# Differential attention with blocks in the order 3, 0, 1, 2, two sets of score banks and the rotation's additions on GpSimd; beside it minima, a folded final norm and an early load

## The chip, the core and the metric

The kernel runs on one core of one Trainium2 chip. The metric is the device time of one launch in microseconds (us). All engines of the core work from queues of their own: TensorE (PE in the rows; PEld is its weight load), VectorE (DVE), ScalarE (ACT), GpSimd (POOL) and SyncE (SP), which only issues transfers here. PEclk in the profile is the granted clock of TensorE as a share of 2.4 GHz, so 0.5 is its lower level of 1.2 GHz.

## The reference

The program is a stack of three model blocks on 512 tokens of width 1024 in float32. Three places in it matter here.

In the first block, 16 meta tokens stand ahead of the 512. Its differential attention has 8 heads; each head has two score maps over the same values, whose difference weighs the values:

```python
s = jnp.einsum('bhqd,bhkd->bhqk', qb, k, preferred_element_type=f32)
s = jnp.where(pos[None, :] <= qpos[:, None], s, neg)
pr = jax.nn.softmax(s, axis=-1).reshape(bsz, DIFF_HEADS, 2, nq, seqlen)
attn_w = pr[:, :, 0] - lam * pr[:, :, 1]
return jnp.einsum('bhqk,bhkd->bhqd', attn_w.astype(v.dtype), v)
```

Queries come in 4 blocks of 128, and q and k are rotated first (`partial_rope`). The second block has a sparse attention (NSA) with three branches per group of queries: compressed keys (31 of them), selected keys, and a window. Each is a softmax with a bias, and the three outputs are added with gates. The third block ends with the whole program's last step, `rmsnorm(x, g_final_3)`: x times the inverse root of its mean square over 1024 channels, times a weight.

## The kernel before

The program is a row of stages. Each stage has its own semaphores and ends in a barrier over all engines. Matmul layers run in `chain`, which takes a list of jobs, streams weight slabs of 512 KB through a ring of buffers, splits each slab into a high and a low part (`whi` on ScalarE, `wlo` on VectorE) and gathers three products per tile in PSUM. A slab can be loaded into a buffer of its own, `ahead`, during the chain before, so that the next chain starts at once; the first chain that uses `ahead` issues this load itself, at its start (L195).

`diff_attention` (L1536 on) works through 8 heads of 4 query blocks, 32 steps `a`. Keys of block b are 16 + 128(b + 1) wide: 144, 272, 400, 528. The two maps e = 0, 1 of a head lie in rows 0 to 63 and 64 to 127 of the rotated operands `rot`. PSUM has two banks for each map (`ps_s[e]`, banks A and B). All engines follow one written order, `lagging()`: a head is five slots, first the rotation of its q and k (`swaps`, L1608, a matmul with a permutation) with the transposition of its values (`values`, L1615), then the four blocks in the order 0, 1, 2, 3. In the slot of step a, TensorE does `scores(a)` (S: L1629 for the 16 meta keys, L1632 for the rest), then `turn(a2)` (T: transposes of weights, L1640 and L1642) for the slot two before, then `weigh(a3)` (Wg: weights times values, L1651 and L1653) for three before. VectorE does `maxima` (M: L1761 takes scores plus mask out of PSUM and the row maximum `top`; L1766 turns the two maxima into the exponent's bias `low`), and one slot later `weights` (W: L1771 to L1778). ScalarE does `powers` (exponent, L1695) and the copies out of PSUM. For the rotation GpSimd multiplies by cosines (L1736, L1737), VectorE multiplies the swapped operand by sines (L1749) and adds the two (L1753). Every block's scores start at the same place, so each pair of score matmuls waits until VectorE has taken the pair before it:

```python
for e in range(2):
    pe.wait_ge(top_ready[e], a)
```

`nsa_attention` (L2096 on) has 48 steps p, three per group. VectorE does the same reduction with a bias (L2276) and `low` (L2280), ScalarE the exponents (`powers`, L2231) and its half of the copies of transposed weights (`turned_weights`, L2239 and L2241); TensorE's transposes (L2169, L2172) wait for both engines' copies of the step before. VectorE joins the three branches (L2302 to L2308).

`rmsnorm` (L491 on) is a stage of its own after the last chain: 8 squares on ScalarE, a sum over channels by matmuls with ones (L542, two halves of each of 8 tiles), mean and root, a reciprocal (L556), 8 products (L559), each followed by its transfer to the output.

Of the kernel before, what the change touches and what calls it, by code (L numbers as in the profile page):

```python
# [12 lines left out]
P = 128  # L13
BANK = 512
# [44 lines left out]
class Job:  # L59
# [15 lines left out]
    def makes_pair(self, n):  # L75
        return self.kind in ("join", "relu2") or (self.kind == "ffn" and n % 2 == 1) or self.fold is not None


class Ahead:


    def __init__(self, nc, memory):
        self.nc, self.memory, self.loaded, self.times = nc, memory, nc.alloc_semaphore("ahead_loaded"), 0

    def take(self):
        if self.times == 0:
            self.place = self.memory.enter_context(self.nc.sbuf_tensor("ahead", [P, 8, P], F32, side="right"))
        self.times += 1
        return self.place, self.loaded, self.times


class Fold:
# [3 lines left out]
    def __init__(self, pair, cols, eps, inner=None, eps_inner=None):  # L96
        self.pair, self.cols, self.eps, self.inner, self.eps_inner = pair, cols, eps, inner, eps_inner

# [5 lines left out]
def chain(nc, ones, jobs, T, norm, pending=None, ring=4, side=None, loads=(), taps=None, restore=None, ahead=None,  # L104
# [39 lines left out]
    for s, f in folds:  # L144
        per = 7 * (2 if f.inner is not None else 1)
        sum_no[s], summed_total = (summed_total, summed_total + per), summed_total + per
        fold_job[s] = slabs[s - 1][0]
    two_norms = any(f.inner is not None for f in stat_at.values())
# [11 lines left out]
    with stage(nc) as s_:  # L160
# [18 lines left out]

        first_in = wbuf[0]  # L180
# [10 lines left out]
        with nc.Block() as block:  # L191
            @block.sync
            def _(sp):
                if ahead is not None and ahead[2] == 1:
                    sp.dma_start(first_in[:], jobs[0].w[0, 0]).then_inc(ahead[1], 16)  # L195
# [9 lines left out]
                if following is not None:  # L205
                    sp.wait_ge(lo_ready, (S - 1) // ring * ring + 1)
                    n = following.shape[3] // -(-following.shape[3] // 8)
                    sp.dma_start(first_in[:, 0:n, :], following[0, 0, :, 0:n, :]).then_inc(ahead[1], 16)

            @block.tensor  # L210
            def _(pe):
# [9 lines left out]
                for s, (j, n, i) in enumerate(slabs):  # L221
# [23 lines left out]
                    if side is not None:  # L245
                        side.pe(pe, s, stat)

            @block.scalar
            def _(act):
# [19 lines left out]
                def folded(f, n, x):  # L269
                    copy(f.pair[0][n], x, ACT.Copy, scale=f.cols[:, n:n + 1]).then_inc(hi_done, 1)  # L270
# [57 lines left out]
                if loads:  # L328
                    act.wait_ge(arrived, 16 * len(loads))

            @block.vector
            def _(dve):
# [28 lines left out]
                def folded(f, n, x, last):  # L361
                    no = sum_no[last][0]
                    dve.wait_ge(hi_done, part["made", fold_job[last], n])
# [78 lines left out]
                for s, (j, n, i) in enumerate(slabs):  # L442
# [12 lines left out]
                    if side is not None:  # L455
                        side.dve(dve, s)

# [31 lines left out]


def rmsnorm(nc, ones, x, weight, out, T, eps, src=None, dst=None):  # L491

    pair = isinstance(out, tuple)
    K = x.shape[1]
    nh, th = halves(T)
    with stage(nc) as s:
        w = s.sb("norm_w", [P, K])  # L500
        sq = s.sb("squares", [P, K, T])
        rstd = s.sb("rstd", [P, T])
        acc = s.ps("sum_squares", [P, nh, BANK])
        loaded, squared, summed = s.sem("loaded"), s.sem("squared"), s.sem("summed")
        mean_ready, root_ready, order, stored = s.sem("mean_ready"), s.sem("root_ready"), s.sem("order"), s.sem("stored")
        ready, hi_ready = s.sem("normed"), s.sem("hi_ready")

        whole = sq if pair else out
        acc_v = acc[:, :, 0:th]
        rstd_v = rstd[:].rearrange("p (h t) -> p h t", h=nh)  # L510
        with nc.Block() as block:  # L511
            @block.sync
            def _(sp):
                sp.dma_start(w[:], weight).then_inc(loaded, 16)
                if src is not None:
                    for k in range(K):
                        sp.dma_start(x[:, k, :], src[:, k, :]).then_inc(loaded, 16)
                if dst is not None:
                    for k in range(K):
                        sp.wait_ge(ready, k + 1)  # L520
                        sp.dma_start(dst[:, k, :], out[:, k, :]).then_inc(stored, 16)
# [3198 lines left out]
```

## Time and profile before

| | |
|---|---|
| Median of 3 runs | 3665.03 us (3663.76 to 3668.27) |
| The profiled execution | 3664.28 us |
| Its span | 3662.5 us |
| Mean granted clock | 0.952 |
| Busy | PE 92%, PEld 75%, DVE 55%, ACT 34%, POOL 6% |
| 731.9 to 856: score loop of differential attention | PE busy 105.4 of 124.2 us |
| 1645 to 1783: NSA attention | PE busy 122.8 of 138.0 us |
| 3638 to 3662.5: the program's end | PE busy 9.0 of 24.5 us |

The time of an execution is that of the launch, and the span is from the first to the last instruction that the profile holds. Busy times of an engine over the whole span mix stages with different limits, so the three stretches that the change touches stand apart.

### The profile page before, as it was taken

The numbers are of one execution on the slowest core, as the hardware profiler recorded it, in microseconds if no ns is written. First come the engines' busy times: TensorE is split into PE (matmuls) and PEld (weight loads), VectorE is DVE, ScalarE is ACT, GpSimd is POOL, SyncE is SP. The second block draws the span as 40 slices with busy tenths as digits, with TensorE's granted clock in tenths as the row PEclk, the third lists the DMA queues.
The fourth block names the chain that finished last, engine by engine and source line by source line (L and its number), as shares of the span: only waits on it lengthen the run. The fifth ranks groups of instructions, "written<-read, shape, count | busy, mean of one in ns | idle before, by whom it ended". The sixth has DMA issues, their size and how long they took to land. (4 is left out here: it accounts for less than half of the span.)

```text
span 3662.5 us, 57266 instructions
## 1 busy us (share of the span) xinstructions
PE 3359.4 (92%) x24193; PEld 2748.0 (75%) x24193; DVE 2023.8 (55%) x3286; ACT 1230.1 (34%) x2142; POOL 212.6 (6%) x174
## 2 busy tenths in 40 slices
PE   7988999988999999888999998979699889999998
PEld 6988888856888887656677776857578587878886
DVE  4885564564355344577546776356736545464342
ACT  4552323254333233214433222234412234333231
POOL 2323230010000000000000000000100020000000
PEclk9998998998999999999999999989799789999999
DMA  4431103101222222620122222312022003232221
GB/s 148 154 134 57 43 23 111 58 1 58 98 92 92 98 92 75 158 61 13 47 81 92 86 87 92 102 52 95 11 92 95 1 2 110 79 106 98 95 95 57
DMA packets 99462, 287.84 MB, mean 79 GB/s; under 512 B 19738, under 2 KB 23962, under 8 KB 97160
## 3 DMA queue, kind: packets, MB, share of 16 engines
q1 hardware_dynamic: 93104, 269.43, 21.6%
q10 hardware_dynamic: 6104, 14.75, 1.6%
q8 instruction: 193, 3.16, 0.4%
q14 instruction: 61, 0.50, 0.0%
HBM read 264.22 MB, written 19.89 MB: 78 GB/s over the span
## 5 line engine op out<-in xcount | busy, mean ns | idle before, releaser
L240 PE MATMUL acc<-h_hi,whi 128*128 128x512 f32 x1992 | 800.3, 402 | 64.8 <-DVE wlo L432 42.4
L240 PE MATMUL acc<-h_hi,wlo 128*128 128x512 f32 x1992 | 791.3, 397 | 0.0
L240 PE MATMUL acc<-h_lo,whi 128*128 128x512 f32 x1928 | 770.0, 399 | 0.0
L240 PEld LDWEIGHTS acc<-h_hi,whi 128*128 128x128 f32 x1992 | 379.1, 190 | 175.3 <-DVE wlo L432 44.7
L338 DVE TENSOR_TENSOR wlo<-wbuf,whi 128x1024 fp32r<-128x1024 f32 (+3 forms) x277 | 318.6, 1150 | 273.4 <-ACT whi L256 271.1
L240 PEld LDWEIGHTS acc<-h_hi,wlo 128*128 128x128 f32 x1992 | 379.3, 190 | 87.9
L240 PEld LDWEIGHTS acc<-h_lo,whi 128*128 128x128 f32 x1928 | 366.7, 190 | 86.1 <-issue 2.9
L256 ACT ACTIVATE whi<-wbuf 128x1024 fp32r<-128x1024 f32 (+3 forms) x277 | 274.5, 991 | 348.1 <-PE acc L240 318.3
L240 PE MATMUL acc<-arena_round,whi 128*128 128x512 f32 x736 | 236.4, 392 | 4.8 <-DVE arena_round L398 4.8
L338 DVE TENSOR_TENSOR wlo<-ahead,whi 128x1024 fp32r<-128x1024 f32 (+3 forms) x132 | 152.3, 1154 | 139.9 <-ACT whi L256 139.2
L256 ACT ACTIVATE whi<-ahead 128x1024 fp32r<-128x1024 f32 (+3 forms) x132 | 131.4, 995 | 174.1 <-PE acc L240 167.7
L240 PEld LDWEIGHTS acc<-arena_round,whi 128*128 128x128 f32 x736 | 139.3, 190 | 34.6 <-DVE arena_round L398 5.6
L240 PE MATMUL acc<-arena_round,wlo 128*128 128x512 f32 x416 | 162.8, 391 | 0.0
L672 PE MATMUL acc<-h_hi,whi 128*128 128x264 f32 x480 | 141.4, 295 | 7.5 <-POOL wlo L660 7.5
L240 PE MATMUL acc<-gates_round,whi 128*128 128x512 f32 x384 | 141.2, 395 | 3.0 <-DVE gates_round L398 1.8
L404 DVE TENSOR_TENSOR x<-acc,x 128x512 f32<-128x512 f32 x64 | 44.3, 691 | 178.2 <-PE acc L240 178.2
L672 PE MATMUL acc<-h_hi,wlo 128*128 128x264 f32 x480 | 137.0, 286 | 0.0
L672 PE MATMUL acc<-h_lo,whi 128*128 128x264 f32 x480 | 137.0, 285 | 0.0
L240 PE MATMUL acc<-gates_round,wlo 128*128 128x512 f32 x320 | 125.4, 392 | 0.0
L289 ACT ACTIVATE val<-tmp 128x512 f32<-128x512 f32 x64 | 40.5, 633 | 216.7 <-DVE tmp L400 216.7
L2837 POOL MEMSET scores<- 128x2048 f32 x1 | 1.8, 1809 | 1768.6 <-POOLq L42 1768.6
L1433 PE MATMUL acc<-h_hi,whi 128*128 128x264 f32 x336 | 103.1, 307 | 1.4 <-DVE wlo L1473 1.4
(752 smaller groups left out, 6349.4 us busy)
## 6 DMA issues: line engine op xcount, KB each, us to landing
wbuf<-in_mlp_out SPq DMA_DIRECT2D x46, 512.0 KB, 3.3
wbuf<-in_mlp_in SPq DMA_DIRECT2D x45, 512.0 KB, 3.2
wbuf<-in_w_gates SPq DMA_DIRECT2D x38, 512.0 KB, 3.3
wbuf<-in_ffn_up SPq DMA_DIRECT2D x29, 512.0 KB, 3.2
wbuf<-in_w_qkv SPq DMA_DIRECT2D x22, 512.0 KB, 3.3
rwkv_factors<-factors SPq DMA_DIRECT2D x8, 1320.0 KB, 4.6
ahead<-in_mlp_in SPq DMA_DIRECT2D x19, 512.0 KB, 3.2
wbuf<-in_w_rwkv SPq DMA_DIRECT2D x18, 512.0 KB, 5.5
```

The source lines that it names most:

```text
L240: mm = nc.tensor.matmul(acc[t % NB][:, 0:T], wt[s % ring][:, k - a, :], xt, start=(kx == 0 and q == 0), stop=(kx == job.K - 1 and q == 2))
L256: copy(whi[s % ring][:, 0:size(s), :], wbuf[s % ring][:, 0:size(s), :], ACT.Copy).then_inc(hi_ready, 1)
L289: copy(val[t % 2][:], tmp[t % 2][:], ACT.Square)
L338: TT(wlo[s % ring][:, 0:size(s), :], wbuf[s % ring][:, 0:size(s), :], whi[s % ring][:, 0:size(s), :].bitcast(F32), ALU.subtract).then_inc( ...
L404: TT(job.dst[n], ps, job.other[n], ALU.add).then_inc(evicted_d, 1)
L672: mm = nc.tensor.matmul(acc[n % 2][:, hf, 0:H], wt[n % R][:, kx, :], xt[:, kx, at], start=(kx == 0 and q == 0), stop=(kx == 7 and q == 2))
L1433: mm = nc.tensor.matmul(acc[n % NB][:, h, 0:H], wt[n % R][:, k, :], xt[:, k, h * H:(h + 1) * H], start=(k == 0 and q == 0), stop=(k == 7 a ...
L2837: nc.gpsimd.memset(scores[:], 0.0).then_inc(cleared, 1)
```

## The change

1. `diff_attention` takes the blocks of a head in the order 3, 0, 1, 2. `place` puts scores at three different starts, so that block 3 takes both banks, 0 bank A, 1 bank B, 2 bank A; a step waits for the block that used its bank last. The rotation of the next head no longer has a slot of its own: it is issued behind the last block's scores of this head and uses bank B alone. The 16 meta keys and values of all heads are rotated and transposed once, at the start (`metas`, `rope_meta`). GpSimd, not VectorE, adds the rotation's two parts.
2. In both attentions the reduction multiplies by minus the scale and takes the minimum, which is the bias itself, so `low` is gone.
3. In `nsa_attention` ScalarE does the copies of step p-2 ahead of the exponents of step p.
4. The `rmsnorm` stage is gone. The last chain takes the squares, their sums and the product with the weight (`Ending`) as it finishes each tile of its last job; what is left behind it is one matmul with ones, mean, root, reciprocal and 8 products, six on VectorE and two on GpSimd.
5. The first use of `ahead` is loaded by `diff_attention`'s SyncE, a stage earlier. The buffer exists from the start, and the program asks for less scratch for DMA descriptors to make room.

```diff
-                    for e in range(2):
-                        h = slice(64 * e, 64 * e + 64)
-                        nc.tensor.matmul(ps_s[e][:, LO:BANK], r[h, 0, j * P:(j + 1) * P], r[h, 1, 0:M], start=True, stop=True)
-                    for e in range(2):
-                        h = slice(64 * e, 64 * e + 64)
-                        nc.tensor.matmul(ps_s[e][:, BANK:LO + keys(a)], r[h, 0, j * P:(j + 1) * P], r[h, 1, M:keys(a)],
-                                         start=True, stop=True).then_inc(sc_ready[e], 1)
+                        h, to = slice(64 * e, 64 * e + 64), place(e, a)
+                        q = r[h, 0, b * P:(b + 1) * P]
+                        free = a if a % NJ < 2 else a - 1
+                        if free > 0:
+                            pe.wait_ge(least_ready[e], free)
+                        nc.tensor.matmul(to[:, 0:M], q, meta[h, i, :], start=True, stop=True)
+                        nc.tensor.matmul(to[:, M:keys(a)], q, r[h, 1, 0:keys(a) - M], start=True, stop=True).then_inc(sc_ready[e], 1)
...
+                swaps(0)
+                metas()
+                values(0)
+                for a in range(NA + 3):
+                    if a < NA:
                         scores(a)
-                    elif i is not None:
-                        swaps(i)
-                        values(i)
-                    if a2 is not None:
-                        turn(a2)
-                    if a3 is not None:
-                        weigh(a3)
+                    if a < NA - 1 and a % NJ == NJ - 1:
+                        swaps(head(a) + 1)
+                        values(head(a) + 1)
+                    if 2 <= a < NA + 2:
+                        turn(a - 2)
+                    if a >= 3:
+                        weigh(a - 3)
...
+                    for e in range(2):
+                        pool.wait_ge(cos_done, 2 * i + e + 1)
+                        pool.wait_ge(sin_done, 2 * i + e + 1)
+                        nc.gpsimd.tensor_tensor(r[:, e, :], r[:, e, :], swapped[e][:], ALU.add).then_inc(rope_done, 1)
...
-                for i, a, a1, _, _ in lagging():
-                    if a is not None:
+                rope(0)
+                rope_meta()
+                for a in range(NA + 1):
+                    if a < NA:
                         maxima(a)
-                    elif i is not None:
-                        rope(i)
-                    if a1 is not None:
-                        weights(a1)
+                    if a < NA - 1 and a % NJ == NJ - 1:
+                        rope(head(a) + 1)
+                    if a >= 1:
+                        weights(a - 1)
...
-                        nc.vector.tensor_tensor_reduce(out=pr[e][p % 3][:, 0:n], in0=ps_s[e][p % 2][:, 0:n], in1=b, scale=1.0, scalar=3 * NEG,
-                                                       op0=ALU.add, op1=ALU.max, accum_out=top[e][:, p:p + 1]).then_inc(top_ready[e], 1)
-                    for e in range(2):
-                        dve.wait_ge(top_ready[e], p + 1)
-                        TS(low[e][:, p:p + 1], top[e][:, p:p + 1], -1.0, None, ALU.mult).then_inc(max_ready[e], 1)
+                        nc.vector.tensor_tensor_reduce(out=pr[e][p % 3][:, 0:n], in0=ps_s[e][p % 2][:, 0:n], in1=b, scale=-1.0, scalar=-3 * NEG,
+                                                       op0=ALU.add, op1=ALU.min, accum_out=least[e][:, p:p + 1]).then_inc(least_ready[e], 1)
...
+                if ending is not None:
+                    no = len(stat_at) + 1
+                    dve.wait_ge(stat_ready, no)
+                    TS(scale[:], stat[0][:, 0:T], 1.0 / (8 * P), ending.eps, ALU.mult, ALU.add).then_inc(var_ready, 1)
+                    dve.wait_ge(root_ready, no)
+                    nc.vector.reciprocal(scale[:], scale[:]).then_inc(scale_ready, 1)
+                    dve.wait_ge(scale_ready, no)
+                    dve.wait_ge(scaled, 8)
+                    for k in by_dve_last:
+                        TT(ends_on[k], ends_on[k], scale[:], ALU.mult).then_inc(last_normed, 1)
```

TensorE's queue before, in the middle of differential attention, from the scores of a head's block 3 to the next head's first transposes (`ps_s<-rot` are scores, `rope_swap` the rotation, `ps_v<-ident,p` the values, `ps_m`, `ps_t<-ident,wt` the T, `ps_o` the Wg):

```order
L1629 MATMUL ps_s<-rot 128x16 x2
L1632 MATMUL ps_s<-rot 128x512 x2
L1640 MATMUL ps_m<-ident,wt 16x128
L1642 MATMUL ps_t<-ident,wt 128x128 x2
L1651 MATMUL ps_o<-vtm,wTm 128x128
L1653 MATMUL ps_o<-vt,wT 128x128
L1608 MATMUL ps_s<-p_next,rope_swap 128x512
L1607 MATMUL ps_s<-p,rope_swap 128x16
L1608 MATMUL ps_s<-p,rope_swap 128x512
L1613 MATMUL ps_s<-ident,p 16x128
L1615 MATMUL ps_v<-ident,p 128x128 x4
L1640 MATMUL ps_m<-ident,wt 16x128
```

The same place in the changed kernel, from the rotation to the second block of the new head:

```order
L1588 MATMUL ps_s<-p_next,rope_swap 128x512
L1588 MATMUL ps_s<-p,rope_swap 128x512
L1594 MATMUL ps_v<-ident,p 128x128 x4
L1620 MATMUL ps_m<-ident,wt 16x128
L1622 MATMUL ps_t<-ident,wt 128x128
L1631 MATMUL ps_o<-vtm,wTm 128x128
L1633 MATMUL ps_o<-vt,wT 128x128 x4
L1610 MATMUL ps_s<-meta,rot 128x16
L1611 MATMUL ps_s<-rot 128x512
L1610 MATMUL ps_s<-meta,rot 128x16
L1611 MATMUL ps_s<-rot 128x512
L1620 MATMUL ps_m<-ident,wt 16x128
```

The rotation now has one whole T and the Wg of block 3 behind it before the next head's scores, the 16-column pieces in it are gone, and the new head starts with the 512-wide scores; the meta part of each map stands right ahead of its main part.

ScalarE's queue before, in the middle of NSA attention, over one group (`pr,total` are exponents, `wT<-ps_t` copies of transposed weights, `o_plain` an output):

```order
L2231 ACTIVATE pr,total<-pr,low 128x384 x2
L2241 ACTIVATE wT<-ps_t 128x256
L2231 ACTIVATE pr,total<-pr,low 128x384 x2
L2239 ACTIVATE wT<-ps_t 31x128
L2231 ACTIVATE pr,total<-pr,low 128x31 x2
L2241 ACTIVATE wT<-ps_t 128x384
L2247 ACTIVATE o_plain<-ps_o 128x128
```

The same place now:

```order
L2244 ACTIVATE o_plain<-ps_o 128x128
L2228 ACTIVATE pr,total<-pr,least 128x31 x2
L2238 ACTIVATE wT<-ps_t 128x256
L2228 ACTIVATE pr,total<-pr,least 128x384 x2
L2236 ACTIVATE wT<-ps_t 31x128
L2228 ACTIVATE pr,total<-pr,least 128x384 x2
L2238 ACTIVATE wT<-ps_t 128x384
```

Each copy stands one step's exponents earlier.

GpSimd's queue at the start of differential attention now:

```order
L1724 TENSOR_TENSOR rot<-p_next,rope_cos 128x512
L1724 TENSOR_TENSOR rot<-p,rope_cos 128x512
L1727 TENSOR_TENSOR meta<-p,rope_cos 128x16 x8
L1731 TENSOR_TENSOR rot<-rot,swapped 128x512 x2
L1724 TENSOR_TENSOR rot<-p_next,rope_cos 128x512
```

Before, it held the two `rot<-p,rope_cos` of each head and nothing else; the eight small products and the two additions per head are new.

## Rows read from the trace of the kernel before

**Rows 1.** Windows: score loop of differential attention (length, busy by engine, clock, DMA).

```profile
731.85:856.00 124.15, 105.38 (x643) 67.00 (x643) 84.06 (x317) 72.38 (x291) 15.24 (x12) 0.93 0.00 1
```

**Rows 2.** Timeline of TensorE, one head: start, length, what, [idle before].

```profile
779.74 0.40 PE L1629 MATMUL ps_s<-rot 64*128 64x16 f32 x4
...
781.07 0.28 PE L1640 MATMUL ps_m<-ident,wt 128*16 128x128 f32 x1 [0.61 <-DVE wt L1778]
...
783.85 0.48 PE L1651 MATMUL ps_o<-vtm,wTm 16*128 16x128 f32 x2
...
785.35 0.40 PE L1629 MATMUL ps_s<-rot 64*128 64x16 f32 x4
...
786.42 0.28 PE L1640 MATMUL ps_m<-ident,wt 128*16 128x128 f32 x1
...
787.85 0.40 PE L1629 MATMUL ps_s<-rot 64*128 64x16 f32 x4 [1.05 <-DVE top L1761]
...
789.60 0.27 PE L1640 MATMUL ps_m<-ident,wt 128*16 128x128 f32 x1 [0.39 <-ACT wT L1704]
...
790.75 1.02 PE L1608 MATMUL ps_s<-p,rope_swap 128*128 128x512 f32 x2
791.61 0.29 PE L1607 MATMUL ps_s<-p,rope_swap 128*128 128x16 f32 x2
...
792.70 0.27 PE L1613 MATMUL ps_s<-ident,p 128*16 128x128 f32 x1
...
793.24 0.27 PE L1640 MATMUL ps_m<-ident,wt 128*16 128x128 f32 x1
...
794.88 0.40 PE L1629 MATMUL ps_s<-rot 64*128 64x16 f32 x4
```

**Rows 3.** Timeline of VectorE, the same head, its last block and the next rotation.

```profile
789.32 0.71 DVE L1761 CUSTOM_DVE_ANT_0 sc<-ps_s,mask 128x528 f32<-128x528 f32 x1 [0.37 <-PE ps_s L1632]
...
790.58 0.27 DVE L1766 TENSOR_SCALAR low<-top 128x1 f32<-128x1 f32 x2
...
791.40 0.92 DVE L1778 SCALAR_TENSOR_TENSOR wt<-sc,share 128x400 f32<-128x400 f32 x1
792.25 1.36 DVE L1749 TENSOR_TENSOR swapped<-ps_s,rope_sin 128x512 f32<-128x512 f32 x2
```

**Rows 4.** Timeline of VectorE, a later head, with GpSimd idle.

```profile
836.17 0.15 DVE L1771 RECIPROCAL inv<-total 128x1 f32<-128x1 f32 x1
...
836.80 0.63 DVE L1778 SCALAR_TENSOR_TENSOR wt<-sc,share 128x400 f32<-128x400 f32 x1
```

**Rows 5.** Timeline of GpSimd, the first of a head's two products with the cosines.

```profile
789.36 1.27 POOL L1736 TENSOR_TENSOR rot<-p,rope_cos 128x512 f32<-128x512 f32 x1 [12.59 <-PE ps_s L1632]
```

**Rows 6.** Timeline, the end of differential attention: last scores and last output copy.

```profile
850.25 1.14 PE L1632 MATMUL ps_s<-rot 64*128 64x512 f32 x4
...
864.14 0.27 ACT L1709 ACTIVATE unscaled<-ps_o 128x128 f32<-128x128 f32 x1
```

**Rows 7.** Timeline, start of the next chain: first load, first use.

```profile
878.01 0.33 SPq L195 DMA_DIRECT2D ahead<-in_w_gates  x1
...
881.33 1.33 ACT L303 ACTIVATE whi<-ahead 128x256 fp32r<-128x256 f32 x4 [4.20 <-DMA ahead<-in_w_gates]
```

**Rows 8.** Waits, 1638 to 1800. Who waits for whom: us in total, times, longest.

```profile
PE ps_t L2172 <- ACT wT L2239: 9.7, 10, 1.2
...
PE ps_t L2169 <- ACT wT L2241: 4.7, 11, 0.7
```

**Rows 9.** Timeline of VectorE, the last eviction.

```profile
3638.17 0.69 DVE L404 TENSOR_TENSOR x<-acc,x 128x512 f32<-128x512 f32 x1 [10.19 <-PE acc L240]
```

**Rows 10.** The chain that ended last, from 3600 on: start, length, what.

```profile
3640.49 8.85 PE sum_squares L542 x16
...
3650.74 3.36 DVE rstd L556
...
3655.55 3.98 DVE x L559 x6
```

More of the change, by code:

```diff
@@ L75, in makes_pair @@
     def makes_pair(self, n):
-        return self.kind in ("join", "relu2") or (self.kind == "ffn" and n % 2 == 1) or self.fold is not None
+        return self.kind in ("join", "relu2") or (self.kind == "ffn" and n % 2 == 1) or isinstance(self.fold, Fold)
 class Ahead:
     def __init__(self, nc, memory):
-        self.nc, self.memory, self.loaded, self.times = nc, memory, nc.alloc_semaphore("ahead_loaded"), 0
+        self.loaded, self.times = nc.alloc_semaphore("ahead_loaded"), 0
+        self.place = memory.enter_context(nc.sbuf_tensor("ahead", [P, 8, P], F32, side="right"))
     def take(self):
-        if self.times == 0:
-            self.place = self.memory.enter_context(self.nc.sbuf_tensor("ahead", [P, 8, P], F32, side="right"))
         self.times += 1
@@ L208, in _ @@
                     sp.dma_start(first_in[:, 0:n, :], following[0, 0, :, 0:n, :]).then_inc(ahead[1], 16)
+                if ending is not None:
+                    for k in range(8):
+                        if k in by_dve_last:
+                            sp.wait_ge(last_normed, by_dve_last.index(k) + 1)
+                        else:
+                            sp.wait_ge(last_pool, 1 if k == 3 else 2)
+                        sp.dma_start(ending.dst[:, k, :], ends_on[k]).then_inc(last_stored, 16)
+                    sp.wait_ge(last_stored, 16 * 8)
+            @block.gpsimd
+            def _(pool):
+                if ending is not None:
+                    pool.wait_ge(scale_ready, len(stat_at) + 1)
+                    pool.wait_ge(scaled, 8)
+                    for k in (3, 6):
+                        nc.gpsimd.tensor_tensor(ends_on[k], ends_on[k], scale[:], ALU.mult).then_inc(last_pool, 1)
             @block.tensor
@@ L246, in _ @@
                         side.pe(pe, s, stat)
+                if ending is not None:
+                    pe.wait_ge(summed, sum_no[S][1])
+                    nc.tensor.matmul(stat[0][:, 0:T], ones[:], sums[0][:], start=True, stop=True).then_inc(stat_ready, 1)
             @block.scalar
@@ L269, in folded @@
                 def folded(f, n, x):
+                    if f is ending:
+                        copy(sums[0][:] if n == 0 else sqx[n % 2][:], x, ACT.Square).then_inc(sq_done, 1)
+                        copy(x, x, ACT.Copy, scale=f.cols[:, n:n + 1]).then_inc(scaled, 1)
+                        return
                     copy(f.pair[0][n], x, ACT.Copy, scale=f.cols[:, n:n + 1]).then_inc(hi_done, 1)
@@ L329, in _ @@
                     act.wait_ge(arrived, 16 * len(loads))
+                if ending is not None:
+                    act.wait_ge(var_ready, len(stat_at) + 1)
+                    copy(scale[:], scale[:], ACT.Sqrt).then_inc(root_ready, 1)
             @block.vector
```

247 lines of the change are left out of this document (101 added, 146 removed).

## The prediction

> **What bounds the kernel now.** I first read the page: TensorE is busy for 92% of the span, so a change is worth only what it takes from TensorE's work or its waits. Then I cut out the stretches that the change touches. In the score loop of differential attention TensorE is busy for 105.4 of 124.2 us, at nine tenths of its clock [rows 1]; in NSA attention for 122.8 of 138.0 (the table above); after 3638 it is nearly idle. No engine is full in the first two; the order of waits sets the pace.
>
> One head shows it [rows 2]. It lasts 794.88 - 779.74 = 15.14 us, and TensorE is idle for 0.61 (waiting for VectorE's weights), 1.05 (for the maxima, that is for the only set of banks) and 0.39 (a copy): 2.05, which leaves 13.09 of its own steps. A step's cost is the distance to the next start, less its idle: S of block 3 is 789.60 - 0.39 - 787.85 = 1.36; T of block 1 and Wg of block 0 together 790.75 - 789.60 = 1.15; a rotation matmul 0.86; Wg of block 3 785.35 - 783.85 = 1.50; T of block 0 787.85 - 1.05 - 786.42 = 0.38; S of block 0 781.07 - 0.61 - 779.74 = 0.72.
>
> **Differential attention, the head.** Two 16-column rotations (0.29, one row, and only one of the pair of operands has it, so 0.14) and one of the five transposes of the values (793.24 - 792.70 = 0.54, so 0.11 each) leave each head: 13.09 - 0.25 = 12.84. Now the new waits, by walking through the four steps:
> - Block 3's pair fills both banks, so block 0's scores wait until VectorE has read it. VectorE starts 0.11 after TensorE's step is over and takes 790.58 - 789.32 = 1.26 [rows 3]; TensorE starts again about 0.23 after a maximum (787.85 shows no more). That is 1.60, and the T and Wg between cover 1.15: idle 0.45.
> - The T after it needs W of block 2, which VectorE does behind that maximum: 836.80 + 0.63 - 836.17 = 1.26 [rows 4], so it is ready 1.37 + 1.26 + 0.12 = 2.75 after the scores of block 3, and TensorE is there after 1.60 + 0.72 = 2.32: idle 0.43.
> - Blocks 1 and 2 find a bank free; I count nothing.
> - The next head needs its rotation. After S of block 2 TensorE does 2 x 0.86 + 0.44 + 0.38 + 1.50 = 4.04. VectorE's maximum of block 2 (528 columns take 1.26, so 400 by width 0.96) ends at 1.1, the two sine products (0.68 each [rows 3]) at 1.8 and 2.5. GpSimd's two additions, priced as its product of the same size, 1.27 [rows 5] and back to back, run from 1.9 to 4.4: idle 0.4 to 0.5.
>
> The head becomes 12.84 + 0.45 + 0.43 + 0.45 = 14.15, 1.0 less. Over the 7 boundaries this saves 7. The two `low` add nothing to it: TensorE's wait for the bank ends with the maximum, before them, and so does the wait counted here; they only shorten the way to the exponent.
>
> **Its ends.** From the last scores of block 3 (850.25 + 1.14) to the last output copy (864.14 + 0.27) pass 13.0 us, at half clock [rows 6]. The last block is now block 2 of 400 keys, with its long predecessor four steps back. M, exponent, W, T, copies and Wg of block 3 are each a quarter to a fifth longer than those of block 2, and the small blocks' steps wait in the shade of it; I take 3, bounds 0 and 4. At the start 16 small matmuls of the meta keys and values stand ahead of the first scores, at half clock, and GpSimd's eight products beside them: I take 1.2 lost, bounds 0.5 and 2.5. Together the part saves 7 + 3 - 1.2 = 9, bounds 0 and 14.
>
> **The price of the additions.** GpSimd's product is 1.27 where VectorE's like it is 0.68, and VectorE's weights of 400 keys take 0.92 beside that product [rows 3] and 0.63 with GpSimd idle [rows 4]. So the two cost each other something like 0.3 where they meet. Now GpSimd's additions meet W of block 1, which has two operands in SBUF. The Trainium skill's SBUF — State Buffer ("two separate sides") goes further: it calls the shared port pair an exclusive lock, which the second one waits for until the first is done. Its GPSIMD Engine Reference (4.1, Engine selection) advises against two-input elementwise work there, at about half the speed. By that rule the second addition ends some 0.5 later and the head boundary costs 0.9, not 0.45. The trace agrees with half speed; whether a whole instruction waits, it doesn't show.
>
> **NSA attention.** TensorE's idle time there is almost all one kind: its transposes wait for ScalarE's copy of the step before, 9.7 + 4.7 us in 21 waits [rows 8]. The copy stands behind the exponents of a younger step, and these behind `low`. The change puts the copy first and drops `low`. The copy's own input is ready long before (TensorE wrote it a step earlier), so it runs when TensorE needs it. What is late next is VectorE: its half of the copies, and in the small groups of the joined branches, where its many short instructions fill the step. I take 12 of 14.4, with bounds 5 (half of the first row) and 15. What ScalarE's exponents lose by standing behind a copy of 0.3 to 0.6 is hidden: they have most of a step until TensorE turns them.
>
> **The program's end.** The last eviction ends at 3638.17 + 0.69 = 3638.86 [rows 9]. Now follow a square (0.7), an addition to the sums (0.7), one matmul with ones (two halves, 8.85 / 8 = 1.1), mean and root (3650.74 - 3640.49 - 8.85 = 1.4) and the reciprocal with its gap, 3.4 [rows 10]: 3646.15. The reciprocal stays whole on the path. Six products of VectorE took 3.98; two of GpSimd's (1.27) run beside them and slow them: all side by side it is 4.0, all one after another 6.5, and I take 5.6, as the weights' 0.92 against 0.63 says that they don't share freely. From the last product's end, 3659.53, to the end of the span are 2.95 now, and stay. The end comes at 3646.15 + 5.6 + 2.95 = 3654.7 instead of 3662.5: 7.8 saved, bounds 6.9 and 9.4; I count 8. Before that, squares and weight products (ScalarE) and sums (VectorE) lie beside matmuls of tiles of 8 slabs; if that cover failed, a late tile's 0.7 would show once.
>
> **The early load.** The next chain's first use of its slab waits from 877.1 for a transfer issued at 878.01, until 881.33 [rows 7]. Issued a stage earlier it is there; ScalarE can start when the transfer was issued before: 3.3 saved, bounds 2.5 and 5, as TensorE's half clock at that chain's start begins and ends earlier with it. The transfer itself, 512 KB in a stage that moves nothing else, costs nothing; smaller descriptor scratch has no queue that uses it here.
>
> **The sum.** 9 + 12 + 8 + 3.3 = 32.3. The profiled execution was 3664.28, its span 1.8 less, and the median of the runs is 0.75 above it. 3664.28 - 32.3 + 0.75 gives 3632.7; I say 3632.5. With the bounds of the terms not all at one end, its own range is 3627 to 3638.
>
> **Rivals.**
> - *The two maps no longer run side by side.* Map 0 and 1 use different halves of the rows, and their two 512-wide matmuls together take 1.14 (the row merges four pieces) [rows 6], where one of full height takes 0.86 each time. The new code puts the meta piece of map 1 between them. If that makes them queue, the pair of block 3 costs 1.72 instead of 1.36 and the head 1.3 more in its four pairs: +10, 3643. Against it: the piece uses map 1's own rows. Chance 0.10.
> - *NSA moves its wait.* VectorE's copy and join take the place of ScalarE's copy, and only 4 of 14.4 are gained: +8, 3640.5. For it: VectorE is busy for most of the small steps. Chance 0.11.
> - *GpSimd is late.* If the second addition first waits for VectorE's weights, which is up to 0.63 [rows 4], or if each takes half as long again as the product's 1.27, the boundary costs 0.6 to 1.3 more, 7 times, 4 to 9: 3637 to 3642, say 3640. For it: the additions end 0.4 after TensorE is there even undisturbed. Chance 0.09. The lock that the Trainium skill's SBUF — State Buffer states would be one way to it.
> - *More is gained.* All of NSA's waits, 9.4 at the end, the small drain, the clock kept through: 3622 to 3626. Chance 0.13.
> - *Slower.* The fused reduction with a minimum and a scale other than 1 stands nowhere in this trace. Were that form to take twice the time, VectorE's four reductions (1.26 for 528 columns, by width 3.2 for the 1344 of a head) would add 3.2 to a head, most of it on the way from bank to bank: +23 for 8 heads, and in NSA, where 48 such pairs stand ahead of the exponents, some +15 and the 12 not gained. That ends at 3682; the sign turns where the form takes about 1.8 times as long. Against it: it is the same instruction with other operators. Chance 0.04.
> - *No change to be measured:* several of the losses at once, 0.03.
>
> **Chances and range.** 0.2% is 7.3 us, about what a measurement of this kernel tells from no change. The forecast has 0.50. Faster by over 0.2% are it, the first three rivals and the fourth, 0.93; within 0.03; slower 0.04. The range takes in the forecast and the first three, 0.80, less their tails, and the upper edge of the fourth: 3623 to 3645.
>
> **What would show it.** TensorE's timeline of a head: a period near 14.15, idle about 0.45 ahead of L1610 of block 0, of the second T, and of the new head; that last one's releaser would be GpSimd's L1731. GpSimd's L1731 at 1.27, and L1724 as before. The custom reduction on VectorE still 0.71 for 528 columns. In NSA no wait of L2166 or L2169 on ScalarE over 3 us in sum. The first slab's `whi` within 1 us of the chain's first instruction. From the last eviction to the end of the span, 16 us. The prediction fails if a head stays at 15, if the reduction is longer, or if NSA's waits come back under another name.

## The result, and the profile after

The changed kernel takes 3659.66 us (median of 11 runs, 3653.32 to 3663.76), the kernel before 3665.6 (median of 11 runs beside it). The ratio is 0.9979, with a 95% interval of 0.997 to 0.9989: 6 us less and not 32. The profiled execution took 3653.76 us, with a span of 3652.0 and a mean granted clock of 0.945, where it was 0.952 before.

Matched points of the two traces say where the time went. Windows of the differential attention, from its first dummy matmul to the first `whi` of the next chain, first of the kernel before, then of the changed one (stretch, length, busy and count of PE, PEld, DVE, ACT and POOL, granted clock, DMA share, GB/s):

```profile
722.95:881.33 158.38, 129.14 (x756) 86.22 (x756) 97.40 (x362) 84.23 (x316) 20.27 (x16) 0.89 0.02 6
```

```profile
716.23:893.13 176.90, 162.36 (x756) 107.56 (x756) 87.14 (x284) 84.29 (x311) 42.50 (x40) 0.72 0.01 4
759.30:766.00 6.70, 5.95 (x40) 4.07 (x39) 4.60 (x15) 4.21 (x18) 3.85 (x3) 1.00 0.00 0
766.00:776.50 10.50, 10.50 (x38) 6.56 (x39) 3.38 (x13) 4.82 (x19) 0.00 (x0) 0.51 0.01 2
776.50:800.30 23.80, 21.45 (x136) 14.16 (x134) 17.02 (x49) 14.53 (x60) 10.29 (x8) 1.00 0.00 1
800.30:810.50 10.20, 10.20 (x34) 5.93 (x34) 3.30 (x12) 4.16 (x16) 0.21 (x1) 0.50 0.00 0
```

The stage has become 18.5 us longer, not 12 shorter, and TensorE, busy for 162 instead of 129 us, did nothing more for it: each of the two traces holds 756 matmuls. What changed is the granted clock, 0.72 instead of 0.89 (0.93 in the loop alone [rows 1]). The last four rows show the pattern: stretches at 2.4 GHz of 7 to 24 us, and between them some at 1.2 GHz, of 10 to 14 us, in which TensorE is busy without a gap. `ending_on_vector` below has the same attention and shows the loss a second time: 176.3 us at 0.73.

The timeline of TensorE in the changed kernel shows the moment at which the clock falls, and behind it a head at the higher level (779.96 to 794.33):

```profile
763.49 0.39 PE L1610 MATMUL ps_s<-meta,rot 64*128 64x16 f32 x2
...
765.29 0.27 PE L1620 MATMUL ps_m<-ident,wt 128*16 128x128 f32 x1 [0.75 <-ACT wT L1686]
...
765.82 0.59 PE L1631 MATMUL ps_o<-vtm,wTm 16*128 16x128 f32 x2
766.34 1.22 PE L1633 MATMUL ps_o<-vt,wT 128*128 128x128 f32 x4
767.49 0.62 PE L1610 MATMUL ps_s<-meta,rot 64*128 64x16 f32 x4
767.94 1.21 PE L1611 MATMUL ps_s<-rot 64*128 64x256 f32 x4
...
779.96 0.41 PE L1610 MATMUL ps_s<-meta,rot 64*128 64x16 f32 x4 [0.40 <-POOL rot L1731]
...
782.51 0.39 PE L1610 MATMUL ps_s<-meta,rot 64*128 64x16 f32 x2
...
784.31 0.27 PE L1620 MATMUL ps_m<-ident,wt 128*16 128x128 f32 x1 [0.75 <-ACT wT L1686]
...
794.33 0.41 PE L1610 MATMUL ps_s<-meta,rot 64*128 64x16 f32 x4 [0.44 <-POOL rot L1731]
```

At the higher level a head lasts 794.33 - 779.96 = 14.37 us, against 15.14 before [rows 2]: the step I had at 14.15. Two waits are left, 0.40 to 0.44 for GpSimd's addition and 0.75 for a copy of ScalarE's. At 765.82 `L1631 x2` takes 0.59, and at 766.34 `L1633 x4` takes 1.22; at full clock they take 0.48 and 0.71: the clock has fallen just behind the scores of block 0, the idle 0.75 and the transposes of block 2. It falls six times in the score loop, near 745.6, 766.0, 800.3, 817.3, 837.8 and 858.3, each time 4 to 6 us behind the first scores of a head, in this idle time or up to 2 us behind it. (The expectation of `old_attention` below counts five.) In the kernel before it falls once in the loop, near 835.8, for 3 us, and in `old_attention`, which has the old order, twice for as long (773.0 and 790.0).

VectorE and GpSimd around a head's boundary, timelines of the changed kernel:

```profile
793.02 1.55 DVE L1773 SCALAR_TENSOR_TENSOR wt<-sc,share 128x272 f32<-128x272 f32 x1
795.83 0.71 DVE L1759 CUSTOM_DVE_ANT_0 sc<-ps_s,mask 128x528 f32<-128x528 f32 x1 [1.25 <-PE ps_s L1611]
```

```profile
791.78 2.50 POOL L1731 TENSOR_TENSOR rot<-rot,swapped 128x512 f32<-128x512 f32 x2 [9.23 <-DVE swapped L1743]
```

The reduction with a minimum takes 0.71 for 528 columns, as the maximum did [rows 3]. GpSimd's additions take 1.25 each, as priced. But VectorE's weights of 272 columns take 1.55 here, 1.15 to 1.55 at all seven boundaries, and 0.50 on average before: they end at 794.57, just behind the second addition at 794.28.

The other parts: from the first transposes of NSA's stage (L2198, now L2195) to TensorE's first wait of 4.83 us in the chain behind it there were 1987.71 - 1638.62 = 349.1 us before and are 1982.88 - 1647.55 = 335.3 now, 13.8 less, and none of the waits of [rows 8] is left. From the last eviction's end to the end of the span there were 3662.5 - 3638.86 = 23.6 us [rows 9] and are 3652.0 - 3633.99 = 18.0. The timeline of the changed kernel's end:

```profile
3633.30 0.69 DVE L446 TENSOR_TENSOR x<-acc,x 128x512 f32<-128x512 f32 x1 [8.80 <-PE acc L265]
...
3635.44 1.12 PE L274 MATMUL stat<-sums,ones 128*128 128x512 f32 x2 [2.17 <-DVE sums L403]
...
3641.37 5.83 DVE L508 TENSOR_TENSOR x<-x,scale 128x512 f32<-128x512 f32 x6
3641.42 3.44 POOL L233 TENSOR_TENSOR x<-x,scale 128x512 f32<-128x512 f32 x2 [638.47 <-DVE scale L504]
3642.09 6.42 SPq L224 DMA_DIRECT2D out_features<-x  x8
```

The first use of the early load, in the changed kernel's timeline:

```profile
893.13 1.33 ACT L335 ACTIVATE whi<-ahead 128x256 fp32r<-128x256 f32 x4 [0.93 <-PEq L42]
```

ScalarE waits for no transfer there [rows 7], only for the barrier.

The remaining difference of the two spans lies ahead of the stage: the changed kernel's profiled execution is 6.7 us earlier at its start (716.23 against 722.95), where the code is the same. In the fourteen profiles of this document the stage starts between 716.2 and 725.0, so the difference goes with the execution; this one is 6 us below its own kernel's median.

### The profile page after: what moved, and what is told of

It is laid out like the page before. It is cut to its first block and busy times, and to the rows that moved or that the text cites. A ratio compares the mean times of both kernels' runs of the same rounds, so it can differ in the third digit from the quotient of the medians.

```text
span 3652.0 us, 57058 instructions
## 1 busy us (share of the span) xinstructions
PE 3375.8 (92%) x24179; PEld 2759.1 (76%) x24179; DVE 2014.1 (55%) x3117; ACT 1237.2 (34%) x2144; POOL 236.2 (6%) x200
## 5 line engine op out<-in xcount | busy, mean ns | idle before, releaser
L373 DVE TENSOR_TENSOR wlo<-ahead,whi 128x1024 fp32r<-128x1024 f32 (+3 forms) x132 | 152.3, 1154 | 133.0 <-ACT whi L284 132.3
```

The lines of the kernel that those rows point to most:

```text
L373: TT(wlo[s % ring][:, 0:size(s), :], wbuf[s % ring][:, 0:size(s), :], whi[s % ring][:, 0:size(s), :].bitcast(F32), ALU.subtract).then_inc( ...
```

## The experiments

My theory after the traces: the new order of the attention lets the granted clock fall, and this costs what the change gains. The rivals: the time is lost elsewhere, or the clock falls for something else in the new attention. A table of all runs first; "stage" is the same stretch as above, from the profile of each. Each ratio is to runs of the kernel before beside it, with its 95% interval.

| kernel | median, us | ratio | stage, us | clock in it |
|---|---|---|---|---|
| before | 3664 to 3667 | 1 | 158.4 | 0.89 |
| changed | 3659.7 | 0.9979 (0.997 to 0.9989) | 176.9 | 0.72 |
| old_attention | 3640.1 | 0.9927 (0.9915 to 0.9939) | 159.5 | 0.86 |
| copy_first | 3635.5 | 0.9919 (0.9903 to 0.9936) | 150.4 | 0.86 |
| filled_idle | 3629.0 | 0.9896 (0.9883 to 0.9909) | 146.5 | 0.92 |
| one_dummy | 3639.3 | 0.9932 (0.9917 to 0.9947) | 156.6 | 0.84 |
| moved_dummies | 3644.6 | 0.9941 (0.9926 to 0.9955) | 163.7 | 0.81 |
| order_3210 | 3622.5 | 0.9877 (0.9862 to 0.9892) | 136.9 | 0.94 |
| additions_on_vector | 3626.3 | 0.9885 (0.9869 to 0.9901) | 142.0 | 0.92 |
| combined | 3623.4 | 0.9881 (0.9866 to 0.9896) | 142.7 | 0.93 |
| best_copies | 3620.3 | 0.9876 (0.9861 to 0.9891) | 138.8 | 0.93 |
| best_additions | 3616.5 | 0.9864 (0.9847 to 0.988) | 132.3 | 0.96 |
| nsa_exponents_first | 3632.7 | 0.991 (0.9895 to 0.9925) | 137.2 | 0.94 |
| ending_on_vector | 3657.9 (one run) | | 176.3 | 0.73 |

**Is it the attention?** `old_attention` puts the function of before back, with one line more, the early load:

```diff
                 sp.dma_start(weight[:], subln).then_inc(loaded, 16)
+                sp.dma_start(ahead.place[:], following[0, 0]).then_inc(ahead.loaded, 16)
```

> The changed kernel with differential attention as before the change (block order, one set of banks, maxima, additions on VectorE), but with the early load in it; NSA, the end and the load stay changed. Theory 1 (the clock): the new order of the attention makes the granted clock fall to its lower level five times in the score loop (0.72 over the stage after the change, 0.93 before), which costs about 28 us; with the old one the stage is 158.4 - 3.3 = 155 us from its first dummy matmul to the next chain's first whi instead of 176.9, and the program takes 3659.7 - 20 = 3640. Rival (the missing time is spread over the program and differs by execution): 3655 to 3662, no change.

It took 3640.1, as the theory had it: the loss is in this one stage, and with the old attention the other parts bring 26 us together (3666.4 for the kernel before beside these runs). The stage itself was 159.5 and not 155, at a clock of 0.86 instead of 0.89; that the clock took back what the early load gives is my reading, which one execution doesn't prove.

**Is it the clock?** `filled_idle` puts three dummy matmuls of 512 columns where TensorE is idle:

```diff
                     if a < NA:
                         scores(a)
+                    if a < NA and a % NJ == 1:
+                        warm(nc, ps_s[0][:, BANK:2 * BANK], busy, 3)
```

> The changed kernel with three dummy matmuls of 512 columns (0.23 us each at full clock) behind the scores of block 0 in each of the 8 heads, in the idle 0.75 us, into a bank that is free there; no wait is changed and no result used. Theory 1a (the clock falls for want of TensorE's activity in that stretch): the clock holds, the period of a head stays 14.4, and the time falls by nearly all of the 28 us, to 3632. Rival 1b (the clock falls for another reason, such as the 64-row scores or the 16-wide pieces of the meta tokens): the time stays at 3660 or rises by up to 5, since at the lower clock the dummies take twice as long and there is no idle time to hide them.

The timeline of TensorE in `filled_idle`:

```profile
791.54 0.41 PE L1610 MATMUL ps_s<-meta,rot 64*128 64x16 f32 x4 [0.43 <-POOL rot L1733]
...
794.09 0.39 PE L1610 MATMUL ps_s<-meta,rot 64*128 64x16 f32 x2
...
795.07 0.98 PE L56 MATMUL ps_s<-h_hi 128*128 128x512 f32 x3
795.90 0.27 PE L1620 MATMUL ps_m<-ident,wt 128*16 128x128 f32 x1
...
805.91 0.41 PE L1610 MATMUL ps_s<-meta,rot 64*128 64x16 f32 x4 [0.43 <-POOL rot L1733]
```

More work, no wait removed, a head of 14.37 as in the changed kernel (791.54 to 805.91), the same two waits but one filled, and 31 us less in all. The stage went from 176.9 to 146.5: this is the price of the clock's falls in the loop, 30.4 us, shown by one edit that touches nothing else. The clock holds from the second head to the last.

**How much must there be, and where?** `one_dummy` has one in the same place instead of three:

> The changed kernel in its own order 3, 0, 1, 2 with one dummy matmul of 512 columns per head in the idle time behind the scores of block 0, instead of three. If the light stretch is only a little too light (the clock falls in it in some heads and not in others): one dummy holds the clock in most heads, 3630 to 3638. If it is far too light: the clock falls nearly as often as without, 3650 to 3660.

`moved_dummies` has the three at the other end of the head, in the wait for the rotation:

```diff
+                    if 0 < a < NA and a % NJ == 0:
+                        pe.wait_ge(least_ready[0], a)
+                        warm(nc, ps_s[0][:, 0:BANK], busy, 3)
                     if a < NA:
                         scores(a)
```

> The changed kernel with the same three dummy matmuls of 512 columns per head, but at the other end of the head: ahead of the scores of block 3, where TensorE waits 0.44 us for the rotation. Theory 1e (the chip looks at each short stretch by itself, so the light stretch around the scores of block 0 must be filled): the clock falls about as often as without them, and each head costs 0.3 more, 3655 to 3664. Rival 1f (what counts is the activity of the head as a whole): it holds as with the dummies in the idle time, 3630 to 3635.

One dummy took 3639.3, 1 us above what the first theory gave; the three at the other end took 3644.6, which lies between what the two theories gave. Three dummies in the one place (0.9896) and in the other (0.9941) are clear of each other's intervals, so the place matters; the moved ones also made a head 14.57 (764.29 to 778.86) instead of 14.37, up to 1.4 us in all. One dummy in the first place and three in the second aren't told apart by their times. In the traces the clock still fell in the loop three times with one dummy and four times with the moved ones (whose profiled execution, 3651.8, was their slowest), against six, and each time 5 to 7 us behind the first scores of a head. That the moved ones help at all says that the stretch around block 0's scores doesn't decide alone; what else counts, no run here shows.

**Is it the idle time or the order?** `copy_first` shortens the idle time without new work, by putting ScalarE's copy ahead of the exponents:

```diff
+                    if 2 <= a < NA + 2:
+                        turned_weights(a - 2)
                     if a < NA:
                         powers(a)
                     if a < NA - 1 and a % NJ == NJ - 1:
                         values(head(a) + 1)
-                    if 2 <= a < NA + 2:
-                        turned_weights(a - 2)
```

> The changed kernel with one edit on ScalarE in differential attention: the copies of the weights of step a-2 stand ahead of the exponents of step a. This takes away the idle 0.75 us that TensorE has after the scores of block 0 in each head, while it waits for such a copy. Theory 1a (the clock falls because the small blocks' steps and this idle time lie next to each other): a head of 14.36 becomes 13.6 and the clock holds through most of the loop: 3659.7 - 28 - 6 = 3626. Rival 1b (the clock falls by the new order whatever waits there): only the waits at full clock are saved, 2 to 4 us, 3656. Rival 2 (exponents come late behind the copies): no gain or a loss of up to 5.

It came out between theory and rival, 3635.5, and with the widest spread of all runs, 3626.4 to 3649.7. Of its six executions the slowest has a mean granted clock of 0.946 over the program and the fastest 0.954, so the spread goes with the clock. A wait of 0.49 is left, now for VectorE's weights (in this kernel's timeline):

```profile
791.35 0.41 PE L1610 MATMUL ps_s<-meta,rot 64*128 64x16 f32 x4 [0.44 <-POOL rot L1731]
...
795.44 0.28 PE L1620 MATMUL ps_m<-ident,wt 128*16 128x128 f32 x1 [0.49 <-DVE wt L1773]
...
805.47 0.41 PE L1610 MATMUL ps_s<-meta,rot 64*128 64x16 f32 x4 [0.43 <-POOL rot L1731]
```

A head is 14.12 at full clock, and in this trace the clock still fell twice in the loop, again behind the scores of block 0. `order_3210` changes one table and nothing else:

```diff
-        BLOCKS = (3, 0, 1, 2)
+        BLOCKS = (3, 2, 1, 0)
```

> The changed kernel with one table changed: the blocks of a head go 3, 2, 1, 0 instead of 3, 0, 1, 2, with the same places in the banks and no dummy matmuls. Theory 1c (the clock falls because in 3, 0, 1, 2 the smallest scores stand beside small transposes and weights: scores of block 0, transposes of block 2, weights of block 1; in 3, 2, 1, 0 each small piece has a large one beside it): the clock holds through most of the loop, about 3632 to 3640. Rival 1d (the clock falls by what the new attention has everywhere: 64-row scores, meta pieces between them, idle time while ScalarE's copy is late): it falls as often, 3655 to 3665.

This was the surprise: 3622.5, 37 us below the changed kernel and 10 below the lower end of my expectation. Its timeline of TensorE:

```profile
789.48 0.41 PE L1610 MATMUL ps_s<-meta,rot 64*128 64x16 f32 x4 [0.19 <-POOL rot L1731]
...
792.47 0.40 PE L1610 MATMUL ps_s<-meta,rot 64*128 64x16 f32 x4
...
793.83 0.27 PE L1620 MATMUL ps_m<-ident,wt 128*16 128x128 f32 x1 [0.21 <-ACT wT L1686]
...
802.88 0.40 PE L1610 MATMUL ps_s<-meta,rot 64*128 64x16 f32 x4 [0.19 <-POOL rot L1731]
```

A head lasts 802.88 - 789.48 = 13.40, the idle time is 0.19 + 0.21, and the clock holds from the second head on. In this order a small piece stands beside a large one: the small scores of block 0 stand ahead of the rotation's two matmuls of 512 columns. ScalarE's copy is nearly in time. The rival (meta pieces and 64-row scores as such) falls: they are all still there. Less idle time and better mixed steps come together in this kernel, and no run parts their shares. Idle time alone doesn't decide it: the kernel before is idle for 2.05 us in a head, up to 1.05 at once [rows 2], and its clock fell once in the loop, where the changed one is idle for 1.19, 0.75 at once, and its clock fell six times. Whether a loop in the order 3, 0, 1, 2 would hold the clock with the 0.40 of idle time that this kernel has, was not tested; with the 0.92 of `copy_first` the clock fell twice.

**GpSimd's additions.** `additions_on_vector` is `filled_idle` with the additions back on VectorE:

```diff
+                    for e in range(2):
+                        dve.wait_ge(sin_done, 2 * i + e + 1)
+                        dve.wait_ge(cos_done, 2 * i + e + 1)
+                        TT(r[:, e, :], r[:, e, :], swapped[e][:], ALU.add).then_inc(rope_done, 1)
```

> The kernel with dummies behind the scores of block 0 (its time was 3629.0, its clock holds, a head lasts 14.37), with the rotation's two additions back on VectorE. Theory 4 (GpSimd's additions end 0.44 after TensorE is ready for the next head's scores): on VectorE they take 0.68 each instead of 1.27, the rotation is ready 1.1 us earlier and the wait of 0.43 ahead of the scores of block 3 is gone, but VectorE's weights of block 1 come 1.3 later, which TensorE needs only a slot after: a head 14.0 to 14.1, 3626. Rival (the weights' delay comes back as a wait of the transposes behind the scores of block 3, of up to 0.9): 3629 to 3633, GpSimd's help is worth something.

3626.3, as the theory said, but 2.7 us are less than the two intervals can tell apart. The traces show the gain: the wait for the rotation is gone, a head is 803.22 - 789.35 = 13.87 instead of 14.37 (stage 142.0 against 146.5), and VectorE's weights of 272 columns are back at 0.50, in its timeline:

```profile
789.76 0.50 DVE L1775 SCALAR_TENSOR_TENSOR wt<-sc,share 128x272 f32<-128x272 f32 x1
```

**The end.** `ending_on_vector` gives VectorE all eight products:

```diff
-    by_dve_last = (0, 1, 2, 4, 5, 7)
+    by_dve_last = tuple(range(8))
```

> The changed kernel with all 8 last products on VectorE and none on GpSimd. In the trace of the changed kernel six products take 5.83 us beside GpSimd's two (3.44), 0.97 each, where VectorE alone took 0.66 each before. Theory 3 (the two engines hinder each other on tensors in SBUF): 8 x 0.66 = 5.3, the first product is ready 0.3 earlier, the output transfers run without a gap, and from the last eviction's end to the span's end there are 15.7 us instead of 18.0. Rival (GpSimd's two save time in spite of it): 18.5 to 19.

```profile
3639.41 0.69 DVE L446 TENSOR_TENSOR x<-acc,x 128x512 f32<-128x512 f32 x1 [8.80 <-PE acc L265]
...
3647.48 4.90 DVE L508 TENSOR_TENSOR x<-x,scale 128x512 f32<-128x512 f32 x8
3648.20 4.54 SPq L224 DMA_DIRECT2D out_features<-x  x8
```

Eight products take 4.90 in a row where six took 5.83 beside GpSimd. From the last eviction's end (3640.10) to the end of the span (3656.1) are 16.0 us against 18.0; 15.7 was expected.

**NSA.** `nsa_exponents_first`, on top of `order_3210`, puts ScalarE's exponents ahead of its copies again (the change's third part undone) and keeps the minima:

> The order 3, 2, 1, 0 (3622.5) with one part of the NSA change undone: ScalarE's exponents stand ahead of its copies again; the minima stay. From the last slab before NSA's stage to the same wait behind it the trace before shows 349.1 us, the changed one 335.3. Theory 5 (the copy's place is what frees TensorE): the minima alone are worth 1 to 3 of the 13.8, and the time is 3633 to 3635. Rival (the removed low lets exponents, and so the copies behind them, come early enough by itself): 3623 to 3627.

3632.7, 10 us above `order_3210` and just below the theory's 3633 to 3635. The waits of its NSA stage:

```profile
PE ps_t L2169 <- ACT wT L2236: 4.0, 5, 0.9
...
PE ps_t L2166 <- ACT wT L2238: 1.0, 3, 0.3
...
PE ps_t L2169 <- ACT wT L2238: 0.2, 1, 0.2
```

The minima alone cut these waits from 15.3 (14.4 in [rows 8]) to 5.2. In time they bring less: the matched stretch is 346.5 us, only 2.6 less than the 349.1 before, as the theory's 1 to 3 had it, and `order_3210` has 333.6. Over the stage's first 154 us the granted clock was 0.99 before and is 0.92 with the minima alone, where it fell twice inside the loop (1665.8 to 1672.8 and 1737.5 to 1747.8); these 17 us cost up to 8.6, which is about what is missing. `order_3210` has 0.96 and no such fall. So NSA's loop also lost the clock when most of its waits went. The copy's place is worth 5 us of waits, and in this execution some 8 more by the clock.

**Better than both.** `combined` (copies first, two dummies, eight products on VectorE, order 3, 0, 1, 2), `best_copies` (order 3, 2, 1, 0, copies first, eight products on VectorE) and `best_additions` (order 3, 2, 1, 0, additions and all products on VectorE):

> Three edits of the changed kernel together: ScalarE's copies ahead of the exponents in differential attention, two dummy matmuls behind the scores of block 0, where 0.49 of idle time is left then, and all eight last products on VectorE. If the clock holds: a head 14.12 instead of 14.37 (2 us in all) and 2.0 less at the end than with dummies alone, 3629 - 4 = 3625. If two dummies are too few, as none were with the copies first (3635.5, between 3626 and 3650): 3630 with a wide spread.

> The changed kernel with the blocks in the order 3, 2, 1, 0 (3622.5 alone), ScalarE's copies ahead of the exponents in differential attention, and all eight last products on VectorE. The trace of the order alone shows a head of 13.40 with two waits left, 0.19 for GpSimd's addition and 0.21 for ScalarE's copy. The copy's wait goes (8 x 0.2 = 1.7) and the end is 2.0 shorter: 3618.8. Rival (the exponents come late behind the copies and the transposes wait for VectorE's weights instead, as the 0.49 with the copies first in the order 3, 0, 1, 2): 3620.5 or a little more.

> The changed kernel with the blocks in the order 3, 2, 1, 0, the rotation's additions on VectorE and all eight last products on VectorE; ScalarE's order as in the changed kernel, no dummies. In the order 3, 0, 1, 2 with dummies the additions on VectorE gained 2.7. Theory 4: the wait of 0.19 for the addition goes, 7 x 0.19 = 1.3, and the end gives 2.0: 3619. Rival (in this order VectorE is nearer to the limit: weights of block 1 come 1.3 later and the transposes wait): 3622 or more.

`combined` came 2 us below its forecast. `best_copies` isn't told apart from the order alone (0.9876 against 0.9877), and its trace has the rival's picture: a head is 13.41 (789.80 to 803.21) as it was 13.40, with 0.36 for VectorE's weights (796.53) in place of the 0.21 for ScalarE's copy. `best_additions` has the lowest median, 3616.5 us, 0.9864 of the kernel before, and 43 us below the changed kernel; its expectation was 3619. Its head is 13.14 (786.42 to 799.56). That it is faster than `best_copies` isn't shown by the times, whose intervals overlap. It has no dummies, and GpSimd does nothing that it didn't do before but the eight small products of the meta keys.

## Why the prediction was wrong

I forecast 32.3 us less and the kernel got 6 less. By its own steps:

- **The head, 14.15 (its terms add up to 14.17): the mechanism right, the place of the waits partly.** At the higher clock it is 14.37. TensorE's own steps were priced right: 14.37 less 0.44, 0.75 and 0.33 leaves 12.85, and I had 12.84. Block 0's scores don't wait 0.45: they wait for each map by itself, and its step is stretched to 784.31 - 0.75 - 782.51 = 1.05 instead of 0.72, by 0.33. The transposes of block 2 wait 0.75 (I had 0.43), and not for VectorE's weights but for a copy of ScalarE's, which does the exponents of block 3 first. The wait for GpSimd is 0.44, as worked out.
- **The step that failed** is "The head becomes 12.84 + 0.45 + 0.43 + 0.45 = 14.15, 1.0 less", where it prices all steps by rows at the higher clock. The change took 2.05 - 1.19 = 0.86 us of idle time out of a head and lost the clock. I had looked at TensorE's idle time only as a cost to be taken away, and read in [rows 1] that the clock was 0.93 without asking what kept it there. The runs showed in its place that the clock fell six times in the loop, which cost 30.4 us (`filled_idle`). With the clock held by dummies the attention and the early load bring 158.4 - 146.5 = 11.9, where I had 9 + 3.3. Of my rivals only "more is gained" had the clock in it ("the clock kept through"), and none had it fall.
- **NSA: 12 forecast, 13.8 measured.** Right in sum. The minima alone take two thirds of the waits, but by the one trace only 2.6 us of the time; the copy's place brings the rest.
- **The end: 8 forecast, 5.6 measured.** The products took 5.83 (5.6 forecast). What failed was "From the last product's end to the end of the span are 2.95 now, and stay": there are 3652.0 - 3647.2 = 4.8. The queue takes the tiles in order, tile 3 behind GpSimd's first product, and issues its eight transfers over 6.42 us (4.54 in `ending_on_vector`). That is about half of it: with all products on VectorE this tail is still 3656.1 - 3652.38 = 3.7. A transfer there takes 2.4 us to land, and 2.1 before (medians); why, no run shows.
- **The early load** is there: ScalarE's first `whi` is idle for 0.93 ahead, not 4.20, and the chain behind starts at the higher clock (1.00 at 892, where it was 0.50 before at 881); from the first `whi` to the chain's next long wait are 579.0 us against 581.2, 2.2 less. This was outside the sum.
- **The rivals.** The maps still run side by side: the pair of block 3 takes 781.25 - 779.96 = 1.29, less than 1.36. The minimum costs what the maximum did. GpSimd was not late by more than I had; it cost VectorE instead.

The rule of the Trainium skill that I weighed (SBUF — State Buffer, "two separate sides": an exclusive lock, the second one waits) agrees with the trace now: the weights start at 793.02, while GpSimd's second addition runs from about 793.0 to 794.28, and end at 794.57, 0.29 after it, although they need 0.50 alone. It is so at all seven boundaries: they end 0.29 to 0.30 behind the second addition, whether they take 1.15 or 1.55. That they are the ones who wait, and not the addition, is why it cost the forecast nothing. The prediction says that the trace before doesn't show a whole wait, but its rows 3 have a first sign of it. VectorE's weights of 400 columns start there at 791.40, take 0.92 and end at 792.32, which is 0.42 behind GpSimd's second product, and alone they need 0.63:

```profile
790.59 1.31 POOL L1737 TENSOR_TENSOR rot<-p,rope_cos 128x528 f32<-128x528 f32 x1
```

The Trainium skill's GPSIMD Engine Reference (4.1, Engine selection) advises against such work on GpSimd at all. The traces of `additions_on_vector` and `ending_on_vector` agree: a head 0.50 shorter, and 2.0 us less at the end.

## What to carry to other kernels

When steps are reordered on an engine whose clock depends on its activity, look for the lightest stretch of the new order, not only for the sum of its waits: here a loop with less idle time in each head made its stage 18.5 us longer. Two cheap probes find it: dummy matmuls put into the idle time (in `filled_idle` a head stayed at 14.37), and other permutations of the same table. Work moved to GpSimd must be counted twice where an instruction of VectorE with two operands in SBUF runs beside it.

## What the runs showed of the hardware

- The granted clock fell in a loop in which TensorE was busy for 21.45 of 23.80 us ahead of the fall, and mostly held (0.93) in the old one at 105.4 of 124.2. The share of busy time in the profile doesn't tell which. It fell, in all six cases, behind the small 64-row and 16-column pieces and in or behind the idle 0.75; in `filled_idle`, with three matmuls of 512 columns there, it held from the second head on, and in `one_dummy`, with one, it fell three times.
- The spread between executions was 23 us in `copy_first` (six, mean clocks 0.946 to 0.954) and 5 in `order_3210` (four, 0.953 to 0.955). That a clock which holds only just shows in this way is my reading.
- An instruction of VectorE with two inputs in SBUF (`scalar_tensor_tensor`, 272 columns) ended 0.29 to 0.30 us behind the end of GpSimd's addition, seven times out of seven, and so took 1.15 to 1.55 us instead of 0.50.
- A fused reduction with minimum and a negative scale takes the same 0.71 us for 528 columns as one with maximum and scale 1.
